# Layer 0's projection: each conditioning tile's matmuls one projection tile later on TensorE

## What is computed

```python
mod = (cond @ ada_w[layer] + ada_b[layer])[:, None, :]
shift_m, scale_m, gate_m, shift_f, scale_f, gate_f = jnp.split(mod, 6, axis=-1)
h = rmsnorm(x, norm_mix_g[layer]) * (1.0 + scale_m) + shift_m
proj = h @ w_in
```

## Time and profile before

| | us |
|---|---|
| Median of 3 runs | 3710.52 |
| Lowest and highest | 3708.89, 3712.21 |
| The profiled execution's own time | 3709.78 |
| Its span | 3708.1 |
| TensorE busy in the span | 3413.2 |
| Layer 0's projection, from F0's first matmul to the last conditioning tile | 51.9 to 216.6 |

### The profile page before, as it was taken

The page is one execution under the profiler, slowest core; times in us unless marked ns, Lnnn a source line. Parts: engine busy times, 40 slices in busy tenths (PEclk is TensorE's granted clock), DMA queues, the critical chain, the costliest instruction groups (busy, mean ns, idle before and its releaser), DMA issues. The chain is left out here.

```text
span 3708.1 us, 46261 instructions
## 1 busy us (share of the span) xinstructions
PE 3413.2 (92%) x17788; PEld 2687.9 (72%) x17788; DVE 1706.4 (46%) x3061; ACT 1131.3 (31%) x1422; POOL 1387.9 (37%) x919
## 2 busy tenths in 40 slices
PE   6988999999967779999897998999999998989998
PEld 5864788878667758888695436888899884358887
DVE  5334343437444457474564642744345746521111
ACT  2244322233411132222322343322344322343222
POOL 2323434344553233434231543344410422444434
PEclk9999999999989989999998998999999998999999
DMA  5520344422200014343110001334444320012221
GB/s 227 192 92 9 117 171 152 169 98 91 79 1 1 1 57 170 131 181 142 46 59 33 1 1 57 145 144 170 153 156 173 115 80 1 1 57 84 104 92 62
DMA packets 54653, 353.52 MB, mean 95 GB/s; under 512 B 5856, under 2 KB 6880, under 8 KB 19424
## 3 DMA queue, kind: packets, MB, share of 16 engines
q1 hardware_dynamic: 54208, 349.25, 25.6%
q10 hardware_dynamic: 288, 2.10, 0.1%
HBM read 349.23 MB, written 2.10 MB: 95 GB/s over the span
## 5 line engine op out<-in xcount | busy, mean ns | idle before, releaser
L387 POOL TENSOR_TENSOR W_LO<-ring,W_HI 128x2048 fp32r<-128x2048 f32 (+1 forms) x177 | 729.8, 4123 | 1092.4 <-ACT W_HI L375 1092.4
L443 PE MATMUL PS<-H_HI,W_HI 128*128 128x512 f32 (+1 forms) x1888 | 715.2, 379 | 27.1 <-DVE H_LO L830 21.0
L445 PE MATMUL PS<-H_HI,W_LO 128*128 128x512 f32 (+1 forms) x1888 | 705.2, 374 | 0.0
L444 PE MATMUL PS<-H_LO,W_HI 128*128 128x512 f32 (+1 forms) x1888 | 704.7, 373 | 0.0
L375 ACT ACTIVATE W_HI<-ring 128x2048 fp32r<-128x2048 f32 (+1 forms) x214 | 366.2, 1711 | 481.7 <-PE PS L433 444.6
L443 PEld LDWEIGHTS PS<-H_HI,W_HI 128*128 128x128 f32 x1888 | 360.8, 191 | 91.5 <-issue 31.9
L445 PEld LDWEIGHTS PS<-H_HI,W_LO 128*128 128x128 f32 x1888 | 360.1, 191 | 63.2
L444 PEld LDWEIGHTS PS<-H_LO,W_HI 128*128 128x128 f32 x1888 | 360.9, 191 | 59.7 <-issue 0.2
L872 DVE SCALAR_TENSOR_TENSOR PS<-ring,SC,PS 128x256 f32<-128x256 f32 x768 | 376.2, 490 | 27.0
L431 PE MATMUL PS<-HID_HI,W_HI 128*128 128x512 f32 (+1 forms) x880 | 325.6, 370 | 4.9 <-DVE W_LO L387 4.0
L433 PE MATMUL PS<-HID_HI,W_LO 128*128 128x512 f32 (+1 forms) x880 | 324.0, 368 | 0.0
(11 more groups left out here) (346 smaller groups left out, 5797.2 us busy)
## 6 DMA issues: line engine op xcount, KB each, us to landing
ring<-w_tiles SPq DMA_DIRECT2D x271, 1024.0 KB, 4.8
ring<-d_tiles SPq DMA_DIRECT2D x80, 704.0 KB, 4.1
X<-xT SPq DMA_DIRECT2D x1, 2048.0 KB, 12.4
WORK<-rope_tables ACTq DMA_DIRECT2D x2, 1024.0 KB, 5.5
outT<-H SPq DMA_DIRECT2D x8, 256.0 KB, 2.2
CN<-consts SPq DMA_DIRECT2D x1, 1379.0 KB, 16.3
X<-ctxT SPq DMA_DIRECT2D x1, 1024.0 KB, 9.1
PR<-params SPq DMA_DIRECT2D x1, 465.5 KB, 3.4
```

The source lines that it names most:

```text
L387: eng.tensor_tensor(W_LO[:, b, 0:w], ring[:, g % SLOTS, 0:w], W_HI[:, b, 0:w].bitcast(F32), ALU.subtract).then_inc(sig("tile_split"), 1)
L443: pe.matmul(to, hi[:, cols(k, j)], x_hi(k), start=k == 0, stop=False)
L444: pe.matmul(to, hi[:, cols(k, j)], x_lo(k), start=False, stop=False)
L445: mm = pe.matmul(to, lo[:, cols(k, j)], x_hi(k), start=False, stop=k == n - 1)
```

## The change

TensorE does F0 and F1 first, then A0, then F2, A1, F3, A2 and so on to F7, A6, A7. From F8 on its order is as before. The order of the loads is not changed. The counts of `tile_done` that others wait for are changed with it: `apart` of A0 to A7 is 3 instead of 4, `earlier` of A16 is 14 instead of 13, and the slot of a conditioning tile at position u (u below 16) is held until `tile_done` is G0 + u + 2.

```diff
-            over_pairs(pe, 8, features, lambda m, v, i: pe_ada_tile(pe, 0, m + ADA_START, v))
+
+            features(0, 0, 0)
+            with pe.Fori(0, 3) as i:
+                for v in range(2):
+                    features(i * 2 + (v + 1), 1 - v, i)
+                    pe_ada_tile(pe, 0, i * 2 + (v + ADA_START), v)
+            features(7, 1, 0)
+            for m in (6, 7):
+                pe_ada_tile(pe, 0, m + ADA_START, m % 2)
             for m in range(8, 12):
                 hi, lo = start(m, m % 2)
...
         def dve_attn_in(dve, chain):
-            over_pairs(dve, 8, lambda m, v, i: dve_ada_tile(dve, 0, "attn_in", m + ADA_START, 2 * v + 1, i, v, chain),
+            over_pairs(dve, 8, lambda m, v, i: dve_ada_tile(dve, 0, "attn_in", m + ADA_START, 2 * v + 1, i, v, chain, apart=3),
                        lambda m, v, i: None, chain, ada_steps(0))
             for m in range(8, 12):
                 for n, u in attn_ada(m):

-                    earlier = 13 if n == 16 else 15 if n == 17 else u - 3
+                    earlier = 14 if n == 16 else 15 if n == 17 else u - 3
...
                 if name in SPLIT and not (side(name) and u % 2):
                     apart = 2 if side(name) else 1
                     return sig("tile_split"), i * (SLOTS // apart) + (SPLIT[name] + u // apart + 1)
-                return tile_done, i * SLOTS + (G0[name] + u + 1)
+                return tile_done, i * SLOTS + (G0[name] + u + (2 if name == "attn_in" else 1))
```

## The result

The change made the kernel slower: 3727.51 us (median of 5, 3725.90 to 3731.29) against 3710.52 (3708.89 to 3712.21), a ratio of 1.0048 with a 95% interval of 1.0037 to 1.0059. I had predicted 3721.8 us, with 3725.5 as the upper end. The direction, the two places and most of the mechanism were right; the size, 17.0 us instead of 11.3, was not. The median lies 2.0 us above the upper end.

The account below looks back on a forecast made before the run. TensorE, busy 92% of 3708.1 us, was taken as the bound. F9 8.65 us late plus 2.7 us of low clock, 11.35 us, on 3710.5 us gave 3721.8 us; range 3717.5 to 3725.5 us.

Parts of the forecast that it names:

- the two places: Layer 0's projection: late loads ahead of F3, F5 and F7, and an 11 us TensorE wait ahead of F9.
- TensorE's order: Layer 0's projection: F1 ahead of conditioning tile A0 starts at 65.25 us, not 81.81; one tile (11.4 us) gained.
- The loads: Projection ring: each F tile needs 14.8 us against 11.39 available; 1.5 us lost per tile, 2.3 of 9.2 us lead left.
- The rival in which the loads keep pace: Projection: F loads arrive within a tile's 11.39 us, F8 at about 155.1; 3712.4 to 3715.1 us; chance 8%.
- The wait for A7's slot: Projection: F9's load is issued only when F8 is done; F9 starts 23.4 us behind F8, 8.65 us late.
- F11 keeps its 15.84 us behind A18: Projection's end: F11's load waits for A19, which F9's end sets, so F11's start behind A18 stays and nothing is won.
- The clock: Behind the idle 11 us ahead of F9, TensorE runs at half speed; 2.7 us lost, bounds 0 and 2.9.
- the rival that the clock falls at every second tile: Projection: 2 us waits ahead of F3, F5 and F7 each bring 1.2 GHz, 13.74 us a tile; 3729.5 us; chance 5%.
- Nothing there can take up the delay: Behind the projection stage all engines meet and output projection loads have landed, so the 11.35 us delay stays whole.

Follow-up runs that it names:

- the held slot alone: Kernel before, TensorE's order unchanged, with only SyncE holding A7's ring slot until projection tile F8 is done: 3721.99 us, ratio 1.0038.

## Why the prediction was wrong

*TensorE's order: right.* F1 at 65.2, the wait for A0 4.75 us (4.65 predicted), F2 at 82.03 (81.81).

*The loads: right in mechanism, and in size from F4 on.* The F tile is ready 14.7 us behind the A two ahead (A1 at 95.59 to F4 at 110.41 is 14.8; A3 at 123.00 to F6 at 137.67 is 14.7); the prediction's sum was 14.8. F3 alone came 1.55 us earlier than its 98.1, and with that the waits moved from F3, F5 and F7, where the prediction had them, to F4, F6 and F8. The run with the loads in TensorE's order shows that the late loads, with the falls of the clock behind their waits, took the lead: with it F8 keeps 10.6 us. (The rival in which the loads keep pace adds up to 155.5 for F8, not 155.1; nothing hangs on it.)

*The wait for A7's slot: right.* F9 starts 24.96 us behind F8. Of this 23.4 were predicted, and 1.5 are F8's own slow stretch. The run with this part alone gave 23.14; in the run without it F9 started 10.6 us earlier, of which some 1.5 is F8 at full clock. That F11 keeps its 15.84 us behind A18 held in the changed kernel (15.92), but not with the held slot alone (14.51).

*The clock: here the prediction failed.* Its step was that "in the present run the idle 1.15 us ahead of F10 and 1.17 ahead of F11 left the tiles at full speed". From these two rows it gave the rival that the clock falls at every second tile 5%, and the sum nothing for it. Two rows were too few: with the held slot 1.16 us ahead of the same F11 was followed by a slow tile. It is what happened, at three waits, ahead of F4, F6 and F8 rather than F3, F5 and F7. The rival's own 3729.5 us was nearer the median than the forecast, but its price, 2.7 us a tile, was too high: it came from a tile behind 15.5 us of idle time, where the clock was low for 5.7 us. Behind a short wait a tile lost 1.5 to 1.6. The ledger against the predicted 11.35: F4 and F6, 1.6 each, put F8 3.0 us later than 161.9; F8 itself lost 1.5; F9 lost 1.5 instead of 2.7; that makes 14.65, and 14.84 were measured. The low clock behind F9's wait was in the prediction; what it left out are the falls ahead of F4, F6 and F8, 4.5 us. The Trainium skill ("TensorE: Matmul & The Clock Gate", "HAM oscillation — how this bites in real kernels") describes waits of about 3 to 5 us for a DMA, ahead of every tile, each of which returns the engine to the slow clock. The trace agrees with the pattern, but shows it behind shorter waits, of 2.27, 2.35 and 2.79 us, and not behind the one of 2.56.

*"Nothing there can take up the delay": not quite, and beside the point.* The stages behind the projection gave some 1 us back by 2700 us, and then took 3.8 more, 3.0 of it by the falls at the waits of 1.84 and 1.78 us: 2.9 us more in sum. The range had no term for this either. Its upper end would have had to be 3729. How near the end the miss lies is partly chance: when the changed kernel was run again, its median was 3726.89 us, but two of its five executions (3721.2 and 3721.6) fell inside the range.

## What to carry to other kernels

When an engine's order is changed, the order of the loads and every count that stands for "this tile is done" change with it; test each count at the first and the last tile of the run, where a uniform offset breaks. Look first for a mend on the engine that is late: here moving VectorE's angles brought 14 us, where reordering TensorE cost 17, and brought 7 once the loads followed. And a gap of 2 us on TensorE can cost more than 2 us: look at the granted clock behind it, and put 1.5 us more into the upper end for each.

## What was not expected of the hardware

The length of a short wait didn't tell whether the clock would fall behind it. In the projection stage of the twelve profiles, waits of 1.04 to 2.56 us went both ways. One of 1.16 us ahead of F11 was followed by a slow tile in the kernel with the held slot (13.1 us), and one of 1.17 us ahead of the same tile wasn't in the kernel before (11.6). When the changed kernel was run again, 2.35 us ahead of F8 was followed by a slow tile (13.1 us), and 2.35 us ahead of F11 wasn't (11.6), in one profile. All six waits of 2.79 to 3.12 us were followed by a slow tile. Far behind, a wait of 1.84 us was followed by 0.68 or by 1.00, with the same work on both sides. So two kernels of this size can differ by about 3 us, 0.1%, by falls of the clock at places that the change doesn't touch; the executions of one kernel differed by more (3721.2 to 3727.5 us).
